# A norm without GpSimd, and an FFN's first pair without a modulation step

## The chip, the cores and the metric

The kernel runs on one core of a Trainium2 chip. The metric is the device time of one execution in microseconds, as the median of three runs. Matrix products run on TensorE (PE), elementwise work on VectorE (DVE), ScalarE (ACT) and GpSimd (POOL); SyncE (SP) issues all the DMA transfers.

## The reference, cut to what matters

Two layers transform 512 image tokens and 256 context tokens of width 1024. Each layer has three sublayers (FFN, token mixer, FFN), and each starts with a norm whose result is scaled and shifted by vectors that come from a condition `c`:

```python
mod = (cond_lat @ w_ada[layer] + b_ada[layer])     # 9 vectors of 1024 for each layer
y = x * rsqrt(mean(x * x) + 1e-6) * norm_w
y = y * (1 + scale) + shift                        # modulate
h = h + 0.5 * gate * (silu(y @ w_gate) * (y @ w_up)) @ w_ffn_out   # FFN, width 2816
```

The mixer holds a Fourier mix, retention, and window attention between two more products. All is float32. `w_ada` is 1024 x 9216 for each layer, and must be read and multiplied too, for the image's and for the context's condition.

## The kernel before, in words

**Layout.** Features lie on the 128 partitions and tokens along them: `h` is 8 tiles (k = 0 to 7) of 128 features x 768 tokens. A float32 product is made of three fast ones: each operand is split into a high part (`xhi`, `whi`, rounded by a cast) and the rest (`xlo`, `wlo`), and `xhi*whi + xlo*whi + xhi*wlo` is summed in PSUM. So every weight tile passes through a chain: DMA to `raw`, ScalarE's cast to `whi` (`split_hi`, L1005), VectorE's subtraction to `wlo` (`split_lo`, L1309), and only then TensorE (`unit`, L637). Weights come in pairs of units (slots 0 and 1). An FFN is done in two halves: an "in" phase of 11 pairs (a gate unit and an up unit), then an "out" phase of 4 pairs; the mixer has a "win" phase of 8 pairs, its own middle part, and a "wo" phase of 4.

**Norms.** There are six, norm 0 to norm 5; norms 0, 2, 3 and 5 lead into an FFN, norms 1 and 4 into a mixer. Each is done in two parts of tokens (0 to 511 and 512 to 767; 256 and 256 in norm 5), each part in 8 tiles. For each tile GpSimd multiplies `h` by `rstd` into `tnorm` (two buffers), ScalarE computes scale and shift into `xfull` (two buffers) and, for even k of part 0, a second time into `xhi`; for the other tiles VectorE casts `xhi` from `xfull` (L1441). VectorE subtracts to `xlo` (L1442). Four hand-overs through two-deep buffers for each tile, then. TensorE's first pair behind a norm (`first_pair`, L704) takes the tiles in as they come (semaphore `s_xn`): tile by tile, three matmuls for each unit. Between them VectorE also adds the last tiles of the sublayer before (L1423), sums their squares (L1432), and splits the first weights.

**Modulation steps.** The 144 tiles of `w_ada` products are spread over the kernel in 64 steps of two (after 16 tiles that are done at the start); `ADA_PAIRS` says at which pairs. A step is: SP loads eight transfers into the four pieces of `ada` (`load_ada`, L478), VectorE sums 16 products (`sum_ada`, L1385 and L1388), and at the end of the pair TensorE folds them over the partitions (`ada_fold`, L652). Two of the four pieces lie where `tnorm` and `xfull` are, so behind a norm SP waits for its last `xlo` before it loads those (`norm_done`).

**Order.** Each engine runs its own list in the order written, and SP's transfers are issued in order too. Nothing but the semaphores ties the engines together. SP issues the step's transfers before the next pair's weights.

## Time and profile before

| | us |
|---|---|
| median of 3 runs (lowest to highest) | 2910.24 (2910.11 to 2912.97) |
| the profiled execution | 2913.79 |
| its span, first to last instruction | 2912.0 |
| TensorE busy in it | 2778.7 (95%) |
| VectorE, ScalarE, GpSimd busy | 1594.4, 740.9, 199.3 |
| mean granted TensorE clock | 0.978 |

A row of the timeline has its start and duration in us from the span's start, then engine, line, operation, output <- inputs, and in brackets how long the engine had been idle and which instruction ended that. A duration covers a pipelined instruction from end to end, so neighbours may overlap. PEclk 1.00 is the full TensorE clock. "ns" is said where it is meant. Norm 2 is the one shown in detail: its first root is taken at 1027 us.

### The profile page before, as it was taken

The numbers are of one execution on the slowest core, as the hardware profiler recorded it, in microseconds if no ns is written. First come the engines' busy times: TensorE is split into PE (matmuls) and PEld (weight loads), VectorE is DVE, ScalarE is ACT, GpSimd is POOL, SyncE is SP. The second block draws the span as 40 slices with busy tenths as digits, with TensorE's granted clock in tenths as the row PEclk, the third lists the DMA queues.
The fourth block names the chain that finished last, engine by engine and source line by source line (L and its number), as shares of the span: only waits on it lengthen the run. The fifth ranks groups of instructions, "written<-read, shape, count | busy, mean of one in ns | idle before, by whom it ended". The sixth has DMA issues, their size and how long they took to land.

```text
span 2912.0 us, 41929 instructions
## 1 busy us (share of the span) xinstructions
PE 2778.7 (95%) x15315; PEld 2352.0 (81%) x15315; DVE 1594.4 (55%) x2687; ACT 740.9 (25%) x1107; POOL 199.3 (7%) x151
## 2 busy tenths in 40 slices
PE   6899999989999979999999799999998999899998
PEld 4788888878749868888888688888886839788887
DVE  5676377453458467734773677347336457533333
ACT  4111111132337231111111311111114246422222
POOL 2000000020131020000000200000002041200000
PEclk8999999999999989999999899999999999999999
DMA  7777377313100147725771477357222300233232
GB/s 223 189 180 175 93 187 187 98 39 101 51 1 1 48 103 187 187 64 146 181 174 57 107 174 180 87 125 186 69 67 82 77 15 1 58 99 103 87 106 88
DMA packets 485788, 319.29 MB, mean 110 GB/s; under 512 B 30588, under 2 KB 481488, under 8 KB 485712
## 3 DMA queue, kind: packets, MB, share of 16 engines
q1 hardware_dynamic: 485712, 318.29, 42.8%
q8 instruction: 45, 0.74, 0.1%
q14 instruction: 31, 0.25, 0.0%
HBM read 316.14 MB, written 2.10 MB: 109 GB/s over the span
## 4 chain that ended last, share of the span: by engine, by line
PE 89%; DVE 6%; ACT 2%; DMA 1%; issue 1%; SPq 1%; DVEq 0%; ACTq 0%
PE pg L637 76%; PE pg L704 3%; PE p L913 2%; DVE xlo L1442 2%; PE pn L897 1%; DVE xhi L1441 1%; PE p L652 1%; PE p L843 1%; PE pg L843 1%; PE pg L866 1%; DMA raw<-in_ffn_w_in 1%; DVE wlo L1309 1%; DVE part L1388 1%; ACT xfull L1083 0%; PE pn L788 0%
## 5 line engine op out<-in xcount | busy, mean ns | idle before, releaser
L637 PE MATMUL pg<-xhi,whi 128*128 128x512 f32 x2880 | 805.0, 348 | 8.4 <-DVE wlo L1309 6.4
L637 PE MATMUL pg<-xhi,wlo 128*128 128x512 f32 x2880 | 800.6, 346 | 0.0
L637 PE MATMUL pg<-xlo,whi 128*128 128x512 f32 x2880 | 798.9, 346 | 0.0
L1005 ACT CAST whi<-raw 128x1024 fp32r<-128x1024 f32 (+1 forms) x288 | 321.7, 1117 | 1096.6 <-PE pg L637 1068.9
L1309 DVE TENSOR_TENSOR wlo<-raw,whi 128x1024 fp32r<-128x1024 f32 (+1 forms) x288 | 382.5, 1328 | 372.4 <-ACT whi L1005 369.7
L637 PEld LDWEIGHTS pg<-xhi,whi 128*128 128x128 f32 x2880 | 459.1, 190 | 78.1 <-DVE wlo L1309 6.9
L637 PEld LDWEIGHTS pg<-xlo,whi 128*128 128x128 f32 x2880 | 457.2, 189 | 70.5
L637 PEld LDWEIGHTS pg<-xhi,wlo 128*128 128x128 f32 x2880 | 457.5, 189 | 69.9
L1388 DVE SCALAR_TENSOR_TENSOR part<-ada,cond,part 128x256 f32<-128x256 f32 x960 | 465.2, 485 | 32.7
L1473 DVE SCALAR_TENSOR_TENSOR h<-pg,gcol,h 128x512 f32 (+1 forms) x118 | 71.4, 639 | 463.7 <-PE pg L637 463.7
L637 PE MATMUL pg<-ahi,wlo 128*128 128x512 f32 x1100 | 306.9, 347 | 0.0
L637 PE MATMUL pg<-ahi,whi 128*128 128x512 f32 x1100 | 306.7, 347 | 0.0
L637 PE MATMUL pg<-alo,whi 128*128 128x512 f32 x1100 | 306.2, 346 | 0.0
L597 POOL TENSOR_TENSOR tnorm<-h,rstd 128x256 f32<-128x256 f32 (+1 forms) x96 | 113.2, 1199 | 1942.4 <-ACT rstd L1070 1900.6
L1242 ACT ACTIVATE gate<-pg 128x768 f32<-128x768 f32 (+1 forms) x88 | 66.8, 759 | 595.1 <-PE pg L637 594.1
L637 PEld LDWEIGHTS pg<-ahi,whi 128*128 128x128 f32 x1100 | 174.6, 188 | 27.8
L637 PEld LDWEIGHTS pg<-ahi,wlo 128*128 128x128 f32 x1100 | 174.5, 188 | 27.5
L637 PEld LDWEIGHTS pg<-alo,whi 128*128 128x128 f32 x1100 | 174.2, 188 | 27.8
L1636 DVE TENSOR_TENSOR gate<-gate,pg 128x768 f32<-128x768 f32 (+1 forms) x88 | 78.1, 887 | 148.4 <-PE pg L637 146.6
L704 PE MATMUL pg<-xhi,whi 128*128 128x256 f32 (+1 forms) x240 | 92.4, 385 | 38.3 <-DVE xlo L1442 38.0
L704 PEld LDWEIGHTS pg<-xhi,whi 128*128 128x128 f32 x240 | 50.8, 212 | 57.7 <-DVE xlo L1442 37.0
L704 PE MATMUL pg<-xlo,whi 128*128 128x256 f32 (+1 forms) x240 | 85.1, 355 | 0.0
(201 smaller groups left out, 2346.1 us busy)
## 6 DMA issues: line engine op xcount, KB each, us to landing
ada<-in_w_ada SPq DMA_DIRECT2D x512, 256.0 KB, 4.2
raw<-in_ffn_w_in SPq DMA_DIRECT2D x176, 512.0 KB, 3.9
raw<-in_ffn_w_out SPq DMA_DIRECT2D x64, 704.0 KB, 4.6
raw<-in_w_in SPq DMA_DIRECT2D x24, 512.0 KB, 3.9
ada_first<-in_w_ada SPq DMA_DIRECT2D x8, 1024.0 KB, 11.9
dft_sb<-in_dft SPq DMA_DIRECT2D x2, 2048.0 KB, 9.7
raw<-in_w_in SPq DMA_DIRECT2D x16, 256.0 KB, 3.5
raw<-in_w_o SPq DMA_DIRECT2D x16, 256.0 KB, 2.8
```

Source lines behind the costliest of these rows:

```text
L597: nc.gpsimd.tensor_tensor(tnorm[:, k % 2, p0:p1], h[:, k, p0:p1], rstd[:, p0:p1], ALU.mult).then_inc(s_t, 1)
L637: last = nc.tensor.matmul(pg[s][:, p0:p1], w[:, s, k], v[:, k, p0:p1], start=(k == 0 and n == 0), stop=(k == kt - 1 and n == 2))
L704: last = nc.tensor.matmul(pg[s][:, c0:c0 + p1 - p0], w[:, s, k], v[:, k, p0:p1], start=(k == 0 and n == 0), stop=(k == kt - 1 and n == 2))
L843: last = nc.tensor.matmul(o[p0:p0 + HD, 0:SEQ], w, sdec[:, r % 2, 0:SEQ], start=(jt == 0), stop=(jt == ret_blocks - 1))
L913: last = nc.tensor.matmul(pa[q // 2 % 2][:, s * HD:(s + 1) * HD], probT[:, q % 2, j * P:(j + 1) * P], vatt[:, kt, s * HD:(s + 1) * HD], st ...
L1005: nc.scalar.copy(whi[:, s, 0:nk], raw[:, s, 0:nk]).then_inc(s_whi[s], 1)
L1242: nc.scalar.activation(gate[:, 0:t], pg[0][:, 0:t], ACT.Silu).then_inc(s_free[0], 1)
L1309: nc.vector.tensor_sub(wlo[:, s, 0:nk], raw[:, s, 0:nk], whi[:, s, 0:nk].bitcast(f32)).then_inc(s_w[s], 1)
L1388: ins = nc.vector.scalar_tensor_tensor(part[:, :], ada[q][:, a], cond2[:, n:n + 1], part[:, :], ALU.mult, ALU.add)
L1442: nc.vector.tensor_sub(xlo[:, k, p0:p1], xfull[:, k % 2, p0:p1], xhi[:, k, p0:p1].bitcast(f32)).then_inc(s_xn, 1)
L1473: last = nc.vector.scalar_tensor_tensor(hv, pg[s][:, p0:p1], gcol[:, col, v:v + 1].rearrange("p o v -> p (o v)"), hv, ALU.mult, ALU.add)
L1636: nc.vector.tensor_tensor(gate[:, 0:t], gate[:, 0:t], pg[1][:, 0:t], ALU.mult).then_inc(s_free[1], 1)
```

## The change

The table of modulation steps has new counts, and no step lies in an FFN's first pair (64 steps as before; it starts one pair later, one step more lies in the first out phase, two more in the last in phase). SP loads the second pair's weights before it waits for the norm. In the norm GpSimd does nothing. VectorE multiplies `h` by the scale column and `rstd` in one instruction into `tnorm` (four buffers now), ScalarE adds the shift and rounds into `xhi`, and VectorE computes `tnorm + shift - xhi` into `xlo` in one instruction. VectorE's list has the next tile's scaling ahead of each `xlo`, and the weights' splits and the adds stand later in it. `xfull` is left for the squares alone.

```diff
-ADA_PAIRS = {(0, 0, 0): (16, 11, 2), (0, 0, 1): (42, 11, 0), (0, 1, 0): (64, 11, 0),
-             (0, 1, 1): (86, 11, 0), (1, 0, 0): (108, 11, 0), (1, 0, 1): (130, 7, 0)}
+ADA_STEPS = {(0, 0, 0): (16, 10, 3), (0, 0, 1): (42, 11, 0), (0, 1, 0): (64, 10, 0),
+             (0, 1, 1): (84, 11, 0), (1, 0, 0): (106, 10, 0), (1, 0, 1): (126, 9, 0)}
...
-        tnorm = place("tnorm", [P, 2, TOK], f32, m0 + TOK * 4)
+        tnorm = place("tnorm", [P, 4, TOK], f32, m0 + TOK * 4)
...
-                    if q == 2 and norm_done is not None:
-                        sp.wait_ge(s_xn, norm_done)
...
-                        elif kind == "in" and hf == 0 and a == 0:
+                            continue
+                        if kind == "in" and hf == 0 and a == 0:
                             load_step(0, b, layer)
-                            a = 1
+                            continue
+                        if kind == "in" and hf == 0 and a == 1 and b is not None:
+                            load_step(1, None, layer)
+                            sp.wait_ge(s_xn, xn_count(m, 1, KD - 1))
+                            load_ada(b, 1, layer)
+                            a = 2
...
-                    pool.wait_ge(s_r, 2 * m + part_ + 1)
-                    for k in range(KD):
-                        if k >= 2:
-                            pool.wait_ge(s_xf, xn_count(m, part_, k - 2))
-                        nc.gpsimd.tensor_tensor(tnorm[:, k % 2, p0:p1], h[:, k, p0:p1], rstd[:, p0:p1], ALU.mult
-                                                ).then_inc(s_t, 1)
...
                             first_pair(i, t)
-                            if b is not None:
-                                ada_fold(b, 0)
                             a = 1
...
-                    for dst in (xfull[:, k % 2, p0:p1], xhi[:, k, p0:p1])[:1 if vector_high(part_, k) else 2]:
-                        last = nc.scalar.activation(dst, tnorm[:, k % 2, p0:p1], ACT.Identity,
-                                                    bias=mod[:, shift + k, v:v + 1], scale=acol[:, k, v:v + 1])
+                    nc.scalar.activation(xhi[:, k, p0:p1], tnorm[:, k % 4, p0:p1], ACT.Identity,
+                                         bias=mod[:, shift + k, v:v + 1]).then_inc(s_xh, 1)
...
+                def scaled(part_, k):
+                    ...
+                    nc.vector.scalar_tensor_tensor(tnorm[:, k % 4, p0:p1], h[:, k, p0:p1], acol[:, k, v:v + 1],
+                                                   rstd[:, p0:p1], ALU.mult, ALU.mult).then_inc(s_t, 1)
                 def low(part_, k):
-                    if vector_high(part_, k):
-                        link(nc.vector.tensor_copy(xhi[:, k, p0:p1], xfull[:, k % 2, p0:p1]))
-                    nc.vector.tensor_sub(xlo[:, k, p0:p1], xfull[:, k % 2, p0:p1], xhi[:, k, p0:p1].bitcast(f32)
-                                         ).then_inc(s_xn, 1)
+                    nc.vector.scalar_tensor_tensor(xlo[:, k, p0:p1], tnorm[:, k % 4, p0:p1],
+                                                   mod[:, shift + k, v:v + 1], xhi[:, k, p0:p1].bitcast(f32),
+                                                   ALU.add, ALU.subtract).then_inc(s_xn, 1)
...
                 for k in range(2, KD):
+                    if k + 1 < KD:
+                        scaled(0, k + 1)
                     low(0, k)
+                scaled(1, 0)
                 for k in range(KD):
+                    if k + 1 < KD:
+                        scaled(1, k + 1)
                     low(1, k)
```

On SP's list, behind the wo phase ahead of norm 2 (`raw` takes weights, `ada_57` to `ada_60` are the four pieces of a step; the wait for the norm stands inside). Before:

```order
L491 DMA raw<-in_ffn_w_in 128x8x128 x2
L478 DMA ada_57<-in_w_ada 64x4x256 x2
L478 DMA ada_58<-in_w_ada 64x4x256 x2
L478 DMA ada_59<-in_w_ada 64x4x256 x2
L478 DMA ada_60<-in_w_ada 64x4x256 x2
L538 UNCONDITIONAL_BRANCH
```

and now:

```order
L487 DMA raw<-in_ffn_w_in 128x8x128 x4
L474 DMA ada_57<-in_w_ada 64x4x256 x2
L474 DMA ada_58<-in_w_ada 64x4x256 x2
L474 DMA ada_59<-in_w_ada 64x4x256 x2
L474 DMA ada_60<-in_w_ada 64x4x256 x2
L538 UNCONDITIONAL_BRANCH
```

The weights of the second pair (two more `raw` transfers) have moved from behind the branch to ahead of the step's eight, and ahead of the wait for the norm.

On VectorE's list, at the start of a norm's first part (here norm 1; norms 2 to 5 have the same order). Before:

```order
L1423 SCALAR_TENSOR_TENSOR h<-pg,gcol,h 128x256
L1432 TENSOR_TENSOR rstd<-rstd,xfull 128x256
L1309 TENSOR_TENSOR wlo<-raw,whi 128x1024
L1423 SCALAR_TENSOR_TENSOR h<-pg,gcol,h 128x256
L1442 TENSOR_TENSOR xlo<-xfull,xhi 128x512
L1432 TENSOR_TENSOR rstd<-rstd,xfull 128x256
L1441 CAST xhi<-xfull 128x512
L1442 TENSOR_TENSOR xlo<-xfull,xhi 128x512
L1309 TENSOR_TENSOR wlo<-raw,whi 128x1024
L1442 TENSOR_TENSOR xlo<-xfull,xhi 128x512
```

and now:

```order
L1405 SCALAR_TENSOR_TENSOR h<-pg,gcol,h 128x256
L1429 SCALAR_TENSOR_TENSOR tnorm<-h,acol,rstd 128x512 x2
L1437 SCALAR_TENSOR_TENSOR xlo<-tnorm,mod,xhi 128x512
L1291 TENSOR_TENSOR wlo<-raw,whi 128x1024
L1429 SCALAR_TENSOR_TENSOR tnorm<-h,acol,rstd 128x512
L1437 SCALAR_TENSOR_TENSOR xlo<-tnorm,mod,xhi 128x512
L1414 TENSOR_TENSOR rstd<-rstd,xfull 128x256
L1405 SCALAR_TENSOR_TENSOR h<-pg,gcol,h 128x256
L1291 TENSOR_TENSOR wlo<-raw,whi 128x1024
L1414 TENSOR_TENSOR rstd<-rstd,xfull 128x256
L1429 SCALAR_TENSOR_TENSOR tnorm<-h,acol,rstd 128x512
L1437 SCALAR_TENSOR_TENSOR xlo<-tnorm,mod,xhi 128x512
```

Each tile has two three-operand instructions on VectorE now (`tnorm`, L1429, and `xlo`, L1437) in place of a subtraction and, for most tiles, a cast; the first sum of squares and the first `wlo` have moved behind the first tiles, and the last add behind the second `xlo`.

## Rows read from the trace of the kernel before

**Rows 1.** The page: busy us (share) and instructions by engine.
```profile
PE 2778.7 (95%) x15315; PEld 2352.0 (81%) x15315; DVE 1594.4 (55%) x2687; ACT 740.9 (25%) x1107; POOL 199.3 (7%) x151
```

**Rows 2.** All waits: who <- whom: us in total, times, longest.
```profile
PE pg L704 <- DVE xlo L1442: 38.0, 34, 4.3
...
PE p L652 <- DVE part L1388: 34.5, 3, 11.8
```

**Rows 3.** PE in norm 2: start us, us, what [idle before <- releaser].
```profile
1040.20 0.79 PE L704 MATMUL pg<-xhi,whi 128*128 128x512 f32 x1 [0.33 <-DVE xlo L1442]
...
1050.88 0.39 PE L704 MATMUL pg<-xlo,whi 128*128 128x512 f32 x1
1051.10 0.39 PE L704 MATMUL pg<-xhi,wlo 128*128 128x512 f32 x1
...
1060.34 0.28 PE L704 MATMUL pg<-xhi,wlo 128*128 128x256 f32 x1
1072.39 1.01 PE L652 MATMUL p<-consts,part 128*128 128x2 f32 x4 [11.77 <-DVE part L1388]
```

**Rows 4.** Timeline of PE, behind norm 0.
```profile
80.64 1.02 PE L652 MATMUL p<-consts,part 128*128 128x2 f32 x4 [11.06 <-DVE part L1388]
```

**Rows 5.** Timeline of SP's queue, end of norm 2.
```profile
1057.09 2.58 SPq L478 DMA_DIRECT2D ada<-in_w_ada  x4
1060.02 1.06 SPq L491 DMA_DIRECT2D raw<-in_ffn_w_in  x2
```

**Rows 6.** Timeline of ACT, norm 2 and behind it.
```profile
1027.56 0.63 ACT L1070 ACTIVATE rstd<-rstd 128x512 f32<-128x512 f32 x1
...
1057.78 0.81 ACT L1242 ACTIVATE gate<-pg 128x768 f32<-128x768 f32 x1 [0.20 <-PE pg L704]
1065.99 1.04 ACT L1005 CAST whi<-raw 128x1024 fp32r<-128x1024 f32 x1 [7.40 <-DMA raw<-in_ffn_w_in]
```

**Rows 7.** Timeline of DVE, norm 2 and behind it.
```profile
1032.04 0.47 DVE L1423 SCALAR_TENSOR_TENSOR h<-pg,gcol,h 128x256 f32<-128x256 f32 x1
1032.43 1.36 DVE L1442 TENSOR_TENSOR xlo<-xfull,xhi 128x512 fp32r<-128x512 f32 x1
...
1056.64 0.42 DVE L1442 TENSOR_TENSOR xlo<-xfull,xhi 128x256 fp32r<-128x256 f32 x1
...
1067.07 1.23 DVE L1309 TENSOR_TENSOR wlo<-raw,whi 128x1024 fp32r<-128x1024 f32 x1 [6.09 <-ACT whi L1005]
```

**Rows 8.** DVE by line and form, whole run: busy us, mean ns | idle.
```profile
L1388 DVE SCALAR_TENSOR_TENSOR part<-ada,cond,part 128x256 f32<-128x256 f32 x960 | 465.2, 485 | 32.7
...
L1442 DVE TENSOR_TENSOR xlo<-xfull,xhi 128x512 fp32r<-128x512 f32 x40 | 47.5, 1194 | 5.8 <-ACT xhi L1083 5.1
...
L1423 DVE SCALAR_TENSOR_TENSOR h<-pg,gcol,h 128x512 f32<-128x512 f32 x8 | 6.0, 750 | 31.6 <-PE pg L704 31.6
```

**Rows 9.** Windows: us; busy us (x) PE, PEld, DVE, ACT, POOL; PEclk, DMA, GB/s.
```profile
1073.40:1092.40 19.00, 19.00 (x102) 16.70 (x102) 11.62 (x22) 1.97 (x3) 0.00 (x0) 0.89 0.79 174
1092.40:1109.50 17.10, 17.10 (x102) 15.01 (x102) 12.37 (x23) 2.80 (x4) 0.00 (x0) 1.00 0.76 185
2541.00:2549.20 8.20, 7.52 (x36) 7.21 (x37) 3.79 (x8) 4.01 (x5) 0.64 (x1) 0.58 0.02 6
```

**Rows 10.** Timeline of DVE, the last of norms 0, 1 and 5.
```profile
64.82 0.42 DVE L1442 TENSOR_TENSOR xlo<-xfull,xhi 128x256 fp32r<-128x256 f32 x1
...
68.24 0.18 DVE L1376 TENSOR_SCALAR lgb<-lg 128x16 f32<-128x16 f32 x1
...
655.36 0.43 DVE L1442 TENSOR_TENSOR xlo<-xfull,xhi 128x256 fp32r<-128x256 f32 x1
...
2543.30 0.43 DVE L1442 TENSOR_TENSOR xlo<-xfull,xhi 128x256 fp32r<-128x256 f32 x1
```

**Rows 11.** Timeline of PE, resume behind norm 4.
```profile
2236.31 0.79 PE L637 MATMUL pg<-xhi,whi 128*128 128x512 f32 x1 [6.44 <-DVE wlo L1309]
```

**Rows 12.** Timeline of ACT, the root of norm 5.
```profile
2521.46 0.42 ACT L1070 ACTIVATE rstd<-rstd 128x256 f32<-128x256 f32 x1
```

More of the change, by code:

```diff
@@ L379, in sq_count @@
             return base + n + 1 + (2 * part if m and n >= KD - 2 else 0)
-        def vector_high(part, k):
-            return part == 1 or k % 2 == 1
         def coef_count(m, k):
@@ L400, in ada_runs @@
             kind, l, m, hf = phases[i][:4]
-            b, first_pairs, second_pairs = ADA_PAIRS.get((l, m % 3 // 2, hf), (0, 0, 0))
-            count = {"in": first_pairs, "out": second_pairs}.get(kind, 0)
-            if kind == "out":
-                b += 2 * first_pairs
+            b, in_steps, out_steps = ADA_STEPS.get((l, m % 3 // 2, hf), (0, 0, 0))
+            skip = 1 if kind == "in" and hf == 0 else 0
+            count = {"in": in_steps, "out": out_steps}.get(kind, 0)
+            b += 2 * (in_steps if kind == "out" else 0) - 2 * skip
             runs, at = [], 0
-            while at < min(count, n):
+            if skip:
+                runs, at = [(0, 1, None, l)], 1
+            while at < min(count + skip, n):
                 layer = (b + 2 * at) // MT
-                end = min(count, n, ((layer + 1) * MT - b) // 2)
+                end = min(count + skip, n, ((layer + 1) * MT - b) // 2)
                 runs.append((at, end, b, layer))
@@ L505, in load_step @@
                         if b is not None:
[L506 removed]
+                            load_ada(b, f, layer)
                 elif kind == "out":
```

72 lines of the change are left out of this document (37 added, 35 removed).

## The prediction

> **What bounds the kernel now.** I read the page's busy times first: TensorE works 2778.7 us of a span of 2912.0 [rows 1], so it is the bound, and only what makes it wait or slows its clock can be won. The view of all waits then names who holds it up: `xlo` of the norms, 38.0 us in 34 waits, and three waits of a fold for VectorE's sums, 34.5 us together [rows 2]. Both lie at the norms, so I read norm 2 as a timeline, engine by engine.
>
> Its root is ready at 1027.56 + 0.63 = 1028.19 [rows 6]. The first `xlo` ends at 1033.79 [rows 7]; TensorE waits for tiles until 1040.20 and has no break from there to part 1 [rows 3]; the last `xlo` ends at 1056.64 + 0.42 = 1057.06 [rows 7], 28.9 us behind the root, and TensorE ends the first pair at 1060.6. Then it stands still for 11.77 us until the fold [rows 3]. Why: two pieces of the step wait for the norm's last `xlo`, so SP issues them at 1057.09, and the second pair's weights behind them at 1060.02 [rows 5]. ScalarE is done with the gate at 1058.59 and waits 7.40 us for those weights [rows 6]; VectorE waits 6.09 us in the middle of the step's sums for ScalarE [rows 7], and TensorE waits for the sums. Behind norm 0 it is the same, 11.06 us [rows 4], and the third of the three waits, behind norm 3, is what is left of the 34.5: 11.7. In the stretch after it, the same pair of units takes 19.0 us at a mean clock of 0.89, against 17.1 at 1.00 one pair later [rows 9]: the idle time costs clock too, 1.9 us.
>
> **The change, part by part.** *No step in the first pair, weights early.* The second pair's weights are issued as soon as their slots are free, some 20 us ahead of need. After the first pair nothing is late but the chain gate, cast, subtraction. With the norm as it was: gate to 1058.59, cast 1.04, subtraction 1.23 [rows 6, 7], with hand-overs 1061.0, against 1073.40 now: 12.4 us, and 1.9 us of clock. Is the sum late in the next pair instead? There the eight transfers start at the norm's end as two pieces do now, and from that point to the fold is 1072.39 - 1057.09 = 15.3 us now, 6 to 7 of them the wait for the weights, which is gone. The fold will come due one pair (17.1 us) plus 3 to 4 us after that point. It is in time.
>
> *The norm.* VectorE now does all but ScalarE's one instruction of a tile. Price of the new two-tensor instruction: 256 columns took 0.485 us with both tensors in SBUF, 512 took 0.750 with one in PSUM [rows 8]. Bounds: 0.69 us or a little less for 512 below, and above the 1.194 that `xlo` takes in the mean now [rows 8]. That mean holds waits for GpSimd: the same 512 columns took 1.36 us at 1032.43 while GpSimd wrote `tnorm`, and with GpSimd gone nothing of that kind is left. I take 0.75 and 0.485. Instructions follow each other closer than they last: 0.47 long, 0.39 apart [rows 7], so 0.67 and 0.40 for each. Norm 2: 16 x 0.67 + 16 x 0.40 = 17.1; two `wlo` at 1.15 = 2.3; two sums and an add = 1.1; about 1 us of waiting at the start, while ScalarE writes the first `xhi` behind a weight cast. Together 21.5 us from the root to the last `xlo`, against 28.9. ScalarE needs some 0.75 us for a tile, below VectorE's 1.34, so it is hidden; in part 1 its tile of 256 columns is near VectorE's 0.80 and may cost a few tenths. TensorE needs 1.36 us for a tile of part 0 (six matmuls 0.22 to 0.23 apart [rows 3]), as VectorE does, so neither gains by being faster still. Last `xlo` at 1049.8, then TensorE's last 27 matmuls, which end 3.5 us behind it now (1060.34 + 0.28, about 0.12 apart [rows 3]): 1053.2. The chain for the second pair starts when the first unit is done, and ends at about 1053.5. Against 1073.40 that is 19.9 us, with the clock 21.8.
>
> *The same for the others.* Norm 3 is norm 2 with a wait of 11.7: 21.6. Norm 1 has norm 2's pattern (last `xlo` 655.36 + 0.43 [rows 10]) and no step behind it: 7.4 us on the `xlo`, some of the half-speed tail besides: 8. Norm 4 does not use part 1 in its first pair, but VectorE must finish it before it splits the next weights: TensorE waits 6.44 us there and resumes at 2236.31 [rows 11]. With the norm 7.2 us shorter and the same chain behind it: 6.7. Norm 5 has only tiles of 256 columns: 32 x 0.40 + 2.3 + 1.1 + 1.0 = 17.2 us from its root at 2521.88 [rows 12], so 2539.1 against 2543.73 [rows 10]; TensorE's tail ran at a clock of 0.58 up to 2549.2 [rows 9]. 6.2 us, some of it clock. Norm 0 waits for the modulation's own folds and transfers in part 0, so only part 1 shortens, about 2 us (last `xlo` at 65.24 now [rows 10]). Behind it VectorE works on the decays, to 68.42 [rows 10], now 2 us earlier, and only then splits the second weights: TensorE resumes at 68.6 and not behind the fold at 81.5 [rows 4]. 12.9 us, and 2 of clock: 15.
>
> *What is added.* Three folds move from a wait to full pairs; a fold lasts 1.01 us behind a wait [rows 3] and, at the full clock and with its neighbours overlapped, half of that or less: -1.5. VectorE's 8 us of sums for a step lie in pairs where it is busy 12.4 of 17.1 us with them [rows 9], so they are hidden. In an out phase a pair lasts 23 us, more room still.
>
> Sum: 15 + 8 + 21.8 + 21.6 + 6.7 + 6.2 = 79.3; less 1.5 = 77.8. I take 4 us off, because in part 1 TensorE will still wait for each tile, and its tail may run at half clock after it, as in norm 5 (27 matmuls 0.21 apart in place of 0.12 are 2.4 us, in one or two norms). So 74. The profiled execution took 2913.79, which makes 2840; the median of the runs lies 3.5 us lower: **2836 us**.
>
> **Clock, by the page.** In norm 5's tail the granted clock is 0.58 after the waits for tiles, behind the fold's wait 0.89 over a pair [rows 9]. The Trainium skill (TensorE: Matmul & The Clock Gate, "HAM oscillation — how this bites in real kernels") says that a kernel whose bursts of matmuls are divided by waits falls back to the low clock again and again. The trace agrees in kind. By that rule part 0 could stay at 1.2 GHz throughout, which speaks against the norm's half of the gain; it is rival A.
>
> **Rivals.**
> *A: the norm's supply is faster, but TensorE is not.* The new order has longer waits at the start (the third `xlo` stands behind two sums, an add and two splits), then tiles at just TensorE's pace. If it takes them at 1.2 GHz, a tile of part 0 costs 2.6 us in place of 1.36, the norm's part 0 lasts as long as now, and only a us is won at each norm. The stall still goes: 12.4 + 1.9 twice and 14 at norm 0 are 43; + 6 - 1.5 = 47, so 2863. For it: rows 9. Against: from 1040.20 to part 1 TensorE put 14 of 16 tiles and units through in 11 us with nothing to wait for [rows 3], and at 1050.88 its matmuls were 0.22 apart, the full rate.
> *B: the wait only moves.* The second pair's fold finds its sums late, because eight transfers (2 MB) and the third pair's weights now come together at the norm's end. Then 9 of 12 us return each time: 77.8 - 27 - 5 of clock = 45, so 2865. Against: the margin of 5 us above.
> *C: slower.* VectorE as the only supplier is too slow. If an instruction with two tensors and a column ran in two passes, 1.4 us for 512 and 0.9 for 256, each norm would take 17 us more than I sum up, 100 in all: 2936. It decides from 77.8 / 6 = 13 us a norm, which is about 1.25 us for 512 columns. Against: 960 such instructions at 485 ns [rows 8]. The Trainium skill (VectorE: DVE Perf Modes, "The perf-mode tier table") has a copy in float32 at twice the rate of a two-tensor operation, and casts are what is given up here; by it the new instruction is at 691 ns for 512 columns, if it goes as a plain addition does. That would shorten my sum by 1 us a norm.
> *D: it doesn't do what it says:* the second weights stay late because of their slots. Then only the norms gain, about 40: 2870. By VectorE's list each slot is free with the first pair's `wlo`, early in part 0, so I give it little.
>
> **How the numbers follow.** Forecast 0.75, A 0.12, B 0.07, C 0.03, D 0.03. The forecast's own range is 2824 to 2850: below, norm 0 better by 3, norms better by 1 to 2 each (the 691 ns); above, an instruction 0.1 us longer (3 us a norm in the large ones) or two more tails at half clock. With half of A and B the range for 8 in 10 is 2822 to 2860. A measurement of this kernel tells 0.2% (6 us) from no change. All cases but C are faster by more: faster 0.96, same 0.01, slower 0.03.
>
> **What would show it.** In the new profile no fold waits for `part` at the three places, and the second pair starts within 1 us of the first pair's end behind norms 1, 2, 3 and 5, within 3 behind norm 0 and 4. `xlo` from `tnorm` takes 0.7 to 0.75 us for 512 columns with no spread; root to last `xlo` 21 to 22 us in norms 1 to 4. Waits of TensorE on `xlo` fall from 38 to some 20 us. PEclk in the pair behind norm 2 is above 0.95. The forecast is wrong if a tile takes VectorE above 1.6 us, if a fold waits in the second pair, or if PEclk stays near 0.5 through part 0.

## The result, and the profile after

The changed kernel took 2838.96 us (median of 4 runs, 2828.34 to 2840.37), the kernel before 2910.39 (2910.11 to 2912.97): a ratio of 0.9745, 95% interval 0.9721 to 0.9769. The forecast was 2836. Taken once more with the third set of experiments below it was 2836.73 (5 runs, 2834.78 to 2838.03), against 2912.44 for the kernel before in the same set: 0.9738 (0.9724 to 0.9751). One run of experiment e3 took 8713.7 us at a mean granted clock of 0.308; it is in no comparison, and its cause is open.

The profiled execution was the fastest of all nine, 2828.34 us with a span of 2826.2. Its page, busy times as in [rows 1]:

```profile
PE 2752.1 (97%) x15315; PEld 2330.4 (82%) x15315; DVE 1567.6 (55%) x2711; ACT 715.6 (25%) x1083; POOL 86.1 (3%) x55
```

GpSimd's norm products are gone from it (199.3 before), and VectorE, which took over work, is busy 27 us less than before. TensorE does the same 15315 matmuls and stands still less. It also needs less time for them: 2778.7 us became 2752.1 (2756.7 in the repeat), while the mean granted clock rose from 0.978 to 0.992 (0.991). So of the 85.8 us by which the span is shorter (78.1 in the repeat) 26.6 (22.0) are shorter matmuls, and the rest are shorter waits. Its waits, in the columns of [rows 2]:

```profile
PE pg L690 <- DVE xlo L1437: 7.1, 18, 1.2
...
PE pg L623 <- DVE wlo L1291: 6.0, 5, 3.6
PE pn L684 <- DVE rstd L1414: 5.8, 5, 1.6
...
PE pg L690 <- DVE wlo L1291: 3.2, 2, 2.1
```

Waits for `xlo` fell from 38.0 to 7.1 us, and no wait for `part` is left of 34.5. What is left at the norms is short: weights, the second part's sum of squares, the first weights of norm 2.

VectorE's new instructions by form (busy us, mean ns | idle), to be held against [rows 8]:

```profile
L1437 DVE SCALAR_TENSOR_TENSOR xlo<-tnorm,mod,xhi 128x512 fp32r<-128x512 f32 x40 | 29.9, 746 | 2.9 <-ACT xhi L1063 1.6
L1429 DVE SCALAR_TENSOR_TENSOR tnorm<-h,acol,rstd 128x512 f32<-128x512 f32 x40 | 29.4, 745 | 1.9 <-ACT rstd L1056 1.8
L1437 DVE SCALAR_TENSOR_TENSOR xlo<-tnorm,mod,xhi 128x256 fp32r<-128x256 f32 x56 | 26.8, 480 | 2.8 <-ACT xhi L1063 2.8
L1429 DVE SCALAR_TENSOR_TENSOR tnorm<-h,acol,rstd 128x256 f32<-128x256 f32 x56 | 26.2, 478 | 0.9 <-ACT rstd L1056 0.9
```

The forecast took 0.75 and 0.485 us, and they are 0.746 and 0.480. In the profile of before the old `xlo` alone took 1.194 in the mean for 512 columns [rows 8].

Norm 2 engine by engine, as [rows 3, 5, 6, 7] show it for before. First ScalarE's root, then VectorE's last `xlo`, then TensorE's first chunk and second pair, then SP's queue:

```profile
997.24 0.63 ACT L1056 ACTIVATE rstd<-rstd 128x512 f32<-128x512 f32 x1
```

```profile
1018.77 0.48 DVE L1437 SCALAR_TENSOR_TENSOR xlo<-tnorm,mod,xhi 128x256 fp32r<-128x256 f32 x1 [0.18 <-ACT xhi L1063]
```

```profile
1001.41 0.76 PE L690 MATMUL pg<-xhi,whi 128*128 128x512 f32 x1 [2.06 <-DVE wlo L1291]
...
1023.11 0.62 PE L623 MATMUL pg<-xhi,whi 128*128 128x512 f32 x2 [0.30 <-DVE wlo L1291]
```

```profile
1001.38 3.55 SPq L487 DMA_DIRECT2D raw<-in_ffn_w_in  x2
1019.28 5.26 SPq L474 DMA_DIRECT2D ada<-in_w_ada  x8
```

From the root's end at 997.87 the last `xlo` comes at 1019.25, 21.4 us later (28.9 before), and the second pair at 1023.11, 25.2 us later. Before, the fold alone stood 44.2 us behind the root (1072.39 - 1028.19), and the second pair 45.1. The second pair's weights are issued at 1001.38, 18 us ahead of the last `xlo`; what waits for the norm's end is only the next step's eight transfers.

The windows (columns of [rows 9]) give the clock: TensorE's first chunks of norm 2, the rest of its start, then short stretches in norms 1, 3 and 4, and last the pair behind norm 2 and the tail of norm 5:

```profile
1001.40:1003.80 2.40, 2.39 (x6) 1.63 (x6) 2.40 (x5) 0.36 (x2) 0.00 (x0) 0.52 0.48 138
1003.80:1006.00 2.20, 1.27 (x4) 0.30 (x2) 2.20 (x4) 1.10 (x3) 0.00 (x0) 0.75 0.34 102
...
619.20:622.60 3.40, 3.40 (x10) 2.63 (x9) 3.40 (x6) 2.59 (x5) 0.00 (x0) 0.50 0.00 0
1574.90:1578.30 3.40, 3.12 (x7) 2.51 (x8) 3.40 (x6) 2.43 (x5) 0.00 (x0) 0.50 0.15 43
2155.20:2162.00 6.80, 5.64 (x13) 4.46 (x14) 2.33 (x2) 1.28 (x2) 0.00 (x0) 0.50 1.00 332
```

```profile
1023.10:1040.60 17.50, 17.49 (x100) 15.23 (x100) 12.38 (x22) 2.88 (x4) 0.00 (x0) 1.00 1.04 222
...
2455.00:2463.00 8.00, 7.44 (x55) 6.55 (x53) 5.46 (x13) 5.57 (x9) 0.00 (x0) 1.00 0.00 0
```

The pair behind the norm runs at the full 2.4 GHz (0.89 of it before), and so does norm 5's tail (0.58 before). Half clock is left for one or two short stretches at each norm: at norm 2's start, 10 us behind the roots of norms 1 and 3, and around the wait behind norm 4. The place is not the same in each execution. In the repeat the same wait of 2.06 us stands at norm 2's start (its root ends at 1006.29), and the clock stays full for another 6 us before it falls:

```profile
1009.80:1015.70 5.90, 3.59 (x11) 1.75 (x11) 5.90 (x10) 2.13 (x4) 0.00 (x0) 1.00 0.55 162
1015.80:1019.10 3.30, 3.10 (x7) 2.48 (x8) 3.30 (x6) 2.35 (x5) 0.00 (x0) 0.50 0.07 21
```

The simplest book-keeping of the gain is from one norm's root to the next. The root's end is the row above, and the same row of the other norms; here those of norms 1, 3 and 4 in the profiled run of the changed kernel, then norms 1 to 4 in the profiled run of its repeat:

```profile
608.43 0.63 ACT L1056 ACTIVATE rstd<-rstd 128x512 f32<-128x512 f32 x1
...
1564.78 0.63 ACT L1056 ACTIVATE rstd<-rstd 128x512 f32<-128x512 f32 x1
...
2132.05 0.63 ACT L1056 ACTIVATE rstd<-rstd 128x512 f32<-128x512 f32 x1
```

```profile
611.66 0.63 ACT L1056 ACTIVATE rstd<-rstd 128x512 f32<-128x512 f32 x1
...
1005.66 0.63 ACT L1056 ACTIVATE rstd<-rstd 128x512 f32<-128x512 f32 x1
...
1573.06 0.63 ACT L1056 ACTIVATE rstd<-rstd 128x512 f32<-128x512 f32 x1
...
2139.98 0.63 ACT L1056 ACTIVATE rstd<-rstd 128x512 f32<-128x512 f32 x1
```

| from root to root, us | before | after | gain | repeat | gain |
|---|---|---|---|---|---|
| start to norm 0's | 35.90 | 35.02 | 0.9 | 37.90 | -2.0 |
| 0 to 1 (holds norm 0) | 590.75 | 574.04 | 16.7 | 574.39 | 16.4 |
| 1 to 2 (norm 1, the mixing) | 401.54 | 388.81 | 12.7 | 394.00 | 7.5 |
| 2 to 3 (norm 2) | 589.92 | 567.54 | 22.4 | 567.40 | 22.5 |
| 3 to 4 (norm 3) | 587.34 | 567.27 | 20.1 | 566.92 | 20.4 |
| 4 to the end (norms 4, 5) | 706.55 | 693.52 | 13.0 | 693.29 | 13.3 |
| span | 2912.0 | 2826.2 | 85.8 | 2833.9 | 78.1 |

The stretches from norm 0's root to norm 1's and from norm 2's root to the end agree to 0.4 us between the two executions of one program. The 8 us by which the first profile is faster lie at the start and in the stretch that holds the mixing. Since the same program has them in one execution and not in the other, they are no part of what the change does.

### The profile page after: what moved, and what is told of

Same layout as the page of the kernel before. It is cut to its first block, busy times and chain, and to the rows that moved or that the text cites. A ratio compares the mean times of both kernels' runs of the same rounds, so it can differ in the third digit from the quotient of the medians.

```text
span 2826.2 us, 41817 instructions
## 1 busy us (share of the span) xinstructions
PE 2752.1 (97%) x15315; PEld 2330.4 (82%) x15315; DVE 1567.6 (55%) x2711; ACT 715.6 (25%) x1083; POOL 86.1 (3%) x55
## 4 chain that ended last, share of the span: by engine, by line
PE 92%; DVE 3%; ACT 2%; issue 1%; SPq 1%; DMA 1%; DVEq 0%; ACTq 0%
PE pg L623 77%; PE pg L690 4%; PE p L899 2%; PE pn L883 1%; DVE xlo L1437 1%; PE pg L829 1%; PE p L829 1%; PE p L638 1%; DVE tnorm L1429 1%; PE pg L852 1%; PE pn L774 1%; PE pg L774 0%; SPq L521 0%; ACT whi L991 0%; DVE wlo L1291 0%
## 5 line engine op out<-in xcount | busy, mean ns | idle before, releaser
L623 PEld LDWEIGHTS pg<-xhi,whi 128*128 128x128 f32 x2880 | 455.5, 188 | 77.2 <-DVE wlo L1291 7.5
L690 PE MATMUL pg<-xhi,whi 128*128 128x256 f32 (+1 forms) x240 | 86.1, 359 | 10.5 <-DVE xlo L1437 7.1
L1646 DVE TENSOR_TENSOR alo<-gate,ahi 128x768 f32 (+3 forms) x88 | 78.5, 892 | 9.7
L587 POOL TENSOR_TENSOR rk_st<-z,rk_st 64x768 fp32r<-64x768 f32 x8 | 16.8, 2103 | 2175.9 <-ACT rq_hi L1102 2175.7
L690 PE MATMUL pg<-xlo,whi 128*128 128x256 f32 (+1 forms) x240 | 81.4, 339 | 0.0
## 6 DMA issues: line engine op xcount, KB each, us to landing
ada_first<-in_w_ada SPq DMA_DIRECT2D x8, 1024.0 KB, 11.8
```

The source lines that it names most:

```text
L623: last = nc.tensor.matmul(pg[s][:, p0:p1], w[:, s, k], v[:, k, p0:p1], start=(k == 0 and n == 0), stop=(k == kt - 1 and n == 2))
L690: last = nc.tensor.matmul(pg[s][:, c0:c0 + p1 - p0], w[:, s, k], v[:, k, p0:p1], start=(k == 0 and n == 0), stop=(k == kt - 1 and n == 2))
L1646: nc.vector.tensor_sub(lo, gate[:, 0:t], hi.bitcast(f32)).then_inc(s_a[m, hf], 1)
```

## The experiments

Twelve runs in four sets; the kernel before ran in each (2911.11, 2911.58, 2912.44, 2910.56 us), and every time is set against the one of its own set. All edits are to the changed kernel unless it is said.

**e1, the new norm alone.** The norm of the change (GpSimd out, four `tnorm`, VectorE's two instructions) with the modulation steps, SP's order and TensorE's fold in the first pair of the kernel before:

```diff
-ADA_STEPS = {(0, 0, 0): (16, 10, 3), ...
+ADA_PAIRS = {(0, 0, 0): (16, 11, 2), ...
...
+                    if q == 2 and norm_done is not None:
+                        sp.wait_ge(s_xn, norm_done)
```

> The new norm alone; the modulation steps stay where they were in the kernel before (a step in each FFN's first pair, its second half loaded behind the norm, the second pair's weights behind that). Theory: in the kernel before the fold in norm 2 started 15.3 us after the norm's last xlo, and the second pair 1 us later; both move with the last xlo, so a faster norm keeps its whole gain. In the changed kernel the second pair starts 3.9 us after the last xlo. So this kernel is slower than the changed one by 12.5 us at each of three norms, 37.5 in all, with about 2 for the slower clock behind the waits: 2877 to 2881, about 31 under the kernel before, with three fold waits of 11 to 12 us. Rival: the fold waits swallow the norm's gain in norms 0, 2 and 3 (they are set by the transfers and not by the last xlo), which leaves norms 1, 4 and 5: 21 us of gain, 2889.

2871.20 us (2867.3 to 2874.06): 39.9 under before, ratio 0.9868 (0.9851 to 0.9885). The three fold waits stand, with their length unchanged:

```profile
PE p L634 <- DVE part L1364: 35.5, 3, 12.0
```

So the wait follows the last `xlo` and does not swallow the norm's gain; the rival (2889) is out. The expected gain was too small by 9: the stretches from root to root gain 5.4 at norm 0, 12.0, 9.6 and 10.2 at norms 1, 2 and 3, where VectorE's 7.4 us alone was counted; the rest was not counted, and it is not placed. The stretch of norm 1 holds the mixing, which differs by 5 us between two executions of one program (table above). And by e1's page a part of this half's gain lies in the matmuls themselves: TensorE is busy 2756.5 us in it, 22.2 less than before, and in e2 (below) 2780.8, no less at all.

**e2, the new steps alone.** The kernel before with the new table, SP's order and no fold in the first pair; its norm as it was. 

> The new modulation steps alone (none in an FFN's first pair, the second pair's weights loaded during the norm); the norm is that of the kernel before, with GpSimd's products. Theory: the second pair starts 3.9 us after the last xlo and not 16.4, three times: 37.5 us, and 2 to 4 for the slower clock behind the waits: 2869 to 2872, no fold wait for part. The two halves add up to the whole of 71.4 us. Rival: the halves overlap or need one another, and this one alone gains under 30 us.

2875.91 us (2874.85 to 2881.45): 35.2 under before, ratio 0.988 (0.9864 to 0.9895). No wait for `part` is left. 35.2 and e1's 39.9 make 75.1; both together gave 71.4 and 75.7. The halves add, to within what two sets differ by. The time is 4 to 7 us above what was expected: from root to root the stretches of norms 0, 2 and 3 gave 11.0, 14.0 and 12.3 us in its profile, which is of the slowest of its four runs, and not 14 each.

**e3, early weights with the fold left in the first pair.** e1 with the second pair's weights issued ahead of the wait for the norm's end:

```diff
                     if q == 2 and norm_done is not None:
+                        if ahead is not None:
+                            ahead()          # load_step(1, None, layer)
                         sp.wait_ge(s_xn, norm_done)
```

> The new norm with the old modulation steps (e1), but the second pair's weights are issued ahead of the wait for the norm's end, as in the changed kernel; only the step's second half and the next step's pieces stay behind it. Theory: in the step VectorE splits the second pair's weights between the step's two halves, so late weights delay the fold too. With early ones the fold follows the transfer of the two pieces (some 5 us) and eight sums (some 4): about 10 us after the last xlo instead of 15.3. The fold wait falls from 11.8 to about 6 us, three times: 2860 to 2865, 16 to 20 us under e1. Rival: the fold waits for the modulation pieces and sums alone, the weights are hidden behind them, and nothing changes against e1.

2859.57 us (2852.88 to 2862.84, three runs): 51.5 under before, ratio 0.9819 (0.9794 to 0.9843), 11.6 under e1. The fold waits:

```profile
75.76 1.01 PE L642 MATMUL p<-consts,part 128*128 128x2 f32 x4 [9.17 <-DVE part L1372]
...
1042.17 1.01 PE L642 MATMUL p<-consts,part 128*128 128x2 f32 x4 [5.61 <-DVE part L1372]
...
1617.25 1.02 PE L642 MATMUL p<-consts,part 128*128 128x2 f32 x4 [4.69 <-DVE part L1372]
```

At norms 2 and 3 they are 5.6 and 4.7 instead of 12.0 and 11.7, as the theory had it. VectorE's lists show it: in e1 it stood 6.30 us for `whi` in the middle of the sums, here it goes on:

```profile
1035.62 3.61 DVE L1364 SCALAR_TENSOR_TENSOR part<-ada,cond,part 128x256 f32<-128x256 f32 x7
1045.53 1.22 DVE L1285 TENSOR_TENSOR wlo<-raw,whi 128x1024 fp32r<-128x1024 f32 x1 [6.30 <-ACT whi L987]
```

```profile
1033.00 3.61 DVE L1372 SCALAR_TENSOR_TENSOR part<-ada,cond,part 128x256 f32<-128x256 f32 x7
1036.52 1.22 DVE L1293 TENSOR_TENSOR wlo<-raw,whi 128x1024 fp32r<-128x1024 f32 x1
```

Norm 0's wait lost only 2.7 of 11.8, where 6 were expected, and not all of the shorter waits came through: the stretches of norms 2 and 3 are 5.3 and 3.1 us shorter from root to root than e1's, with waits shorter by 6.4 and 7.1. The clock behind a wait of 4.7 us was as low as behind one of 11.7 (0.86 and 0.91 over a pair), so a wait cut to half costs its tail all the same; the rest has no row. So half or more of the fold wait at norms 2 and 3 was late weights, by way of VectorE's list.

**e4, late weights without the fold.** The other way round:

```diff
-                            load_step(1, None, layer)
                             sp.wait_ge(s_xn, xn_count(m, 1, KD - 1))
+                            load_step(1, None, layer)
                             load_ada(b, 1, layer)
```

> The changed kernel, with the second pair's weights issued behind the wait for the norm's end instead of ahead of it; still no step in the first pair. Theory: the weights are then issued at the last xlo, take 3 to 5 us to land and 2.2 to be split, and the second pair starts 6 to 8 us after the last xlo and not 3.9: 2 to 4 us more at each of three norms, 2845 to 2851. Rival: only the step in the first pair mattered, and this kernel takes what the changed one does, 2839.

2842.86 us (2842.55 to 2849.23), ratio 0.9772 (0.9757 to 0.9788): 3.9 over the changed kernel's first set and 6.1 over its repeat, 2 us under the shortest time that was expected. The second pair waits for `wlo` 2.74, 2.60 and 2.33 us behind norms 0, 2 and 3, in place of 1.61, 0.30 and 0.22. So SP's order alone is worth 4 to 6 us by the medians once no fold stands there, and some 12 while one does (e3 against e1). The profiled run, 4.9 us over this kernel's median, has more: its stretches of norms 0, 2 and 3 are 11.8 us longer than the repeat's.

**e5, GpSimd beside the norm.** GpSimd multiplies 256 columns into scratch, in step with the norm; nothing waits for it. The edit does so in norms 1 to 4 (96 instructions, 97 us), not in norm 5 as its text says; in the kernel before, the norm products took 113 us in six norms:

```diff
+                        for _ in range(2 - part_):
+                            nc.gpsimd.tensor_tensor(scratch, dist_sb[:, 0:256], consts[:, 0:256], ALU.mult
+                                                    ).then_inc(s_beside, 1)
```

> The changed kernel, with GpSimd multiplying tiles of 256 columns into a scratch tile during norms 1 to 5 (two for each chunk of a norm's first part, one in the second, each behind the last chunk's low part); nothing waits for it. Theory: what the change takes off VectorE's path is the time in which both engines read SBUF: in the kernel before the low parts of 512 columns took 0.69 to 1.8 us, mean 1.19, beside GpSimd's products, here 0.74 to 0.75. So VectorE's instructions in the norms grow to about 1.0 to 1.2 us while GpSimd runs, the last xlo comes 4 to 6 us later after the root than 21.4, and the kernel takes 12 to 25 us more, 2851 to 2864. Rival: VectorE's and GpSimd's instructions don't hinder one another, the spread of before was a wait for tnorm and xfull inside the record, and this kernel takes 2839.

2872.23 us (2867.83 to 2875.99), ratio 0.9869 (0.9854 to 0.9884): 39.4 under before, so 36 of the change's 75.7 are gone through an engine that nobody waits for. VectorE and GpSimd in norm 2 (from its root to its last `xlo`, 31.2 us in place of 21.4):

```profile
L1453 DVE SCALAR_TENSOR_TENSOR tnorm<-h,acol,rstd 128x512 f32<-128x512 f32 x8 | 8.8, 1110 | 1.8 <-ACT rstd L1080 1.8
L1461 DVE SCALAR_TENSOR_TENSOR xlo<-tnorm,mod,xhi 128x512 fp32r<-128x512 f32 x8 | 8.7, 1099 | 0.0
L1461 DVE SCALAR_TENSOR_TENSOR xlo<-tnorm,mod,xhi 128x256 fp32r<-128x256 f32 x8 | 7.1, 893 | 0.0
```

```profile
L603 POOL TENSOR_TENSOR cond<-dist_sb,consts 128x256 f32<-128x256 f32 x24 | 24.3, 1012 | 112.0 <-ACT rstd L1080 104.6 <-DVE xlo L1461 6.1
```

The direction was right and the size too small by half: 0.745 us became 1.10, 0.480 became 0.6 to 0.9, 10 us a norm. Norm 5, without the extra GpSimd work, keeps its 0.480. The rival (no hindrance) is out. What in the chip makes the one engine slow the other is not shown by this run.

**e6, another order in norms 1 to 5.** TensorE takes `whi*xhi` as soon as `xhi` is there and `xlo` last, both halves chunk by chunk; VectorE splits the first weights ahead of `xlo`:

```diff
+                for n, (w, v) in enumerate(((whi, xhi), (wlo, xhi), (whi, xlo))):
...
+                    if s == 0 and n != 1:
+                        pe.wait_ge((s_xh, s_xh, s_xn)[n], xn_count(m, part_, k))
...
+                        order = ahead + [(s, k) for k in range(len(ahead) // 2, KD) for s in range(2)]
```

> The changed kernel with another order in norms 1 to 5: TensorE starts a chunk on whi*xhi as soon as xhi is there and needs xlo only for the third product; the two halves of a pair alternate by chunk; VectorE splits the first weights ahead of xlo's first chunk, and does the second part's squares one chunk later. Theory: from the root on, TensorE had 17.2 us of products left and ended 24.9 to 26.1 us after the root in norms 2 and 3, though the last xlo came after 21.4; the rest is waits at the start (2.1, 0.6, 0.6, 0.4 us in norm 2; 1.2 us for the sum of squares in the others) and the half with s=1 that runs behind the last xlo. The first pair's end comes to 22 us after the root: 2.5 to 4 us in each of norms 1, 2 and 3, 1 in 5, none in 4: 8 to 12 us, 2827 to 2831. Rival: VectorE sets the end in any order, only the last 0.5 to 1 us of TensorE can be taken, and the gain is under 4 us.

2835.47 us (2832.49 to 2836.9), ratio 0.9736 (0.9723 to 0.9749): 76.1 under before, where the changed kernel is 75.7 under it. No gain that can be told. The first pair did get shorter as the theory had it, and its clock stays at 1.00 through all of norm 2's first pair (window of this run, columns as above), where the changed kernel had a stretch at half clock. The second window is the start of the second pair:

```profile
1003.00:1025.20 22.20, 20.16 (x111) 16.37 (x109) 20.77 (x37) 14.02 (x24) 0.00 (x0) 1.00 0.16 49
1027.10:1033.80 6.70, 5.55 (x17) 4.78 (x18) 6.49 (x10) 0.78 (x1) 0.00 (x0) 0.50 1.12 234
```

It ended 22.2 us behind the root. But then:

```profile
1028.25 1.01 PE L623 MATMUL pg<-xhi,whi 128*128 128x512 f32 x2 [3.02 <-DVE wlo L1302]
```

Root to second pair is 25.3 us, the 25.2 of the changed kernel to a tenth. And the half clock is not saved, it has moved behind this wait: the third pair starts 45.2 us behind the root, against 42.8 and 43.7 in the two profiles of the changed kernel. With both halves ending together the first weight slot comes free only at the pair's end, and ScalarE's table load and Silu, its cast and VectorE's subtraction follow, which the half with s=1 had hidden before:

```profile
1023.90 1.28 ACT L1233 ACT_TABLE_LOAD   x1
1025.19 0.81 ACT L1233 ACTIVATE gate<-pg 128x768 f32<-128x768 f32 x1
1025.90 1.98 ACT L1003 CAST whi<-raw 128x1024 fp32r<-128x1024 f32 x2
```

The time speaks for the rival, the reason was another: the start of the second pair is set by the chain behind the last `xlo`, and not by TensorE's order in the first pair.

**e7, second weights split earlier.** In norm 4 they are split between the norm's two parts, in norm 0 ahead of the decays:

```diff
+                    norm(i - 1, m, (lambda: (evict(0), evict(1))) if early else None)
...
+                    if between is not None and k in (0, 2):
+                        between(k // 2)          # split_lo(i, s, 1)
```

> The changed kernel with the second pair's weights split earlier where TensorE waited for them: in norm 4 between the norm's two parts (the first two tiles take the first part alone), in norm 0 ahead of the decays. Theory: the two waits for wlo of 3.6 and 1.6 us go, 4 to 5 us in all: 2834 to 2835. Rival: the wait in norm 4 is the norm's second part by another name; VectorE's 6.6 us of it then come before the third pair, and it only moves.

2837.95 us (2836.73 to 2846.93), ratio 0.9745 (0.9732 to 0.9759): nothing gained. The wait behind norm 4 went and the one behind norm 0 fell from 1.62 to 0.31 us, and a new one came before norm 4's third pair:

```profile
2186.62 0.80 PE L623 MATMUL pg<-xhi,whi 128*128 128x512 f32 x1 [11.99 <-DVE wlo L1299]
```

SP's queue names it: the third pair's weights stand behind the norm's end, the rope table and the transform table (2 MB):

```profile
2172.33 0.37 SPq L545 DMA_DIRECT2D rope_sb<-in_rope  x1
2172.74 0.47 SPq L547 DMA_DIRECT2D dft_sb<-in_dft  x1
2173.25 5.32 SPq L487 DMA_DIRECT2D raw<-in_w_in  x2
```

The profiled run (2846.93) is the slowest of the five, 9 us over the median. So the trace shows where the wait comes from, but how long it is in the other four runs isn't known.

**e8, e6 and e7 together.**

> Both edits of e6 and e7 in one kernel. Theory: they touch different waits and add up: 12 to 16 us under the changed kernel, 2823 to 2827. Rival: in norm 4 both take the same wait, and the sum falls short by 2 to 3 us.

2842.89 us (2838.59 to 2843.15), ratio 0.9757 (0.9744 to 0.977), 7 above e6 and 5 above e7, where 12 to 16 under the changed kernel were expected. Each of the two brought its own new wait (3.0 us for `wlo` behind norms 2 and 3, 9.2 before norm 4's third pair), and both stayed.

**e9, e6 mended by its trace.** The half with s=1 runs one chunk behind in the second part; in the first step the weights are split ahead of Silu; the decays stand behind that step:

```diff
+                        if first:
+                            split_hi(nxt, 0, jn)
                         nc.scalar.activation(gate[:, 0:t], pg[0][:, 0:t], ACT.Silu).then_inc(s_free[0], 1)
-                        split_hi(nxt, 0, jn)
+                        if not first:
+                            split_hi(nxt, 0, jn)
```

> e6 with three changes where its trace showed the new wait: in the second part TensorE's half with s=1 runs one chunk behind the half with s=0 (not beside it), so the first weight slot comes free with the last chunk; ScalarE splits the second pair's weights before it takes the gate's Silu in the first step; the decays stand behind the first step. Theory: what sets the second pair's start is the chain last xlo, last chunk with s=0 (0.4), weights split by ScalarE (1.04) and VectorE (1.2), about 2.8 us instead of the 3.9 of the changed kernel and the same of e6, where Silu (0.8) stood in it: 1 us in five norms, and 1.6 in norm 0: 2830 to 2834. Rival: the transfer of the weights or the end of the half with s=1 takes its place, and the time is e6's, 2835.

2831.05 us (2829.21 to 2838.37), ratio 0.9723 (0.9709 to 0.9738): 5.7 under the changed kernel of the same set, as forecast in size (the two intervals overlap, so the difference is only just to be told), but not where: root to second pair at norm 2 is still 25.3 us, now waiting for the gate:

```profile
1026.68 0.86 PE L623 MATMUL pg<-xhi,whi 128*128 128x512 f32 x2 [2.71 <-ACT gate L1235]
```

```profile
1023.37 1.05 ACT L1004 CAST whi<-raw 128x1024 fp32r<-128x1024 f32 x1 [1.12 <-PE pg L697]
1024.43 1.28 ACT L1235 ACT_TABLE_LOAD   x1
1025.73 0.81 ACT L1235 ACTIVATE gate<-pg 128x768 f32<-128x768 f32 x1
```

ScalarE's table load had lain in a wait and now lies in the chain. By the roots 3.9 us are norm 0's (570.5 us from its root to norm 1's, against 574.4). Part of that can be scatter: e5, whose norm 0 is the changed kernel's, has 571.6 there. The rest can't be placed, since the profiled run (2836.99) was 6 us over this kernel's median. A table load placed behind the last `xhi` could take up to 1.3 us out of this chain at norms 2, 3 and 5, an estimate from the row of its 1.28 us; that was not tried.

**e10, two passes.** VectorE's first instruction of a chunk done as two:

```diff
-                    nc.vector.scalar_tensor_tensor(tnorm[:, k % 4, p0:p1], h[:, k, p0:p1], acol[:, k, v:v + 1],
-                                                   rstd[:, p0:p1], ALU.mult, ALU.mult).then_inc(s_t, 1)
+                    link(nc.vector.tensor_tensor(tn, h[:, k, p0:p1], rstd[:, p0:p1], ALU.mult))
+                    nc.vector.tensor_scalar(tn, tn, acol[:, k, v:v + 1], None, ALU.mult).then_inc(s_t, 1)
```

> The changed kernel with VectorE's first instruction of each chunk, (h*acol)*rstd, done as two: h*rstd, then times acol, each waiting for the one before. Theory: from the root to the last xlo VectorE is the bound, so each us that it gets there is a us of the kernel. A tensor_tensor of 512 columns takes 0.69 us and a tensor_scalar of 256 columns 0.35 against 0.48 for the scalar_tensor_tensor; with the wait between, a chunk of 512 columns costs about 0.65 more and one of 256 about 0.36: 8 us more at norms 1 to 4, 5 to 6 at norms 0 and 5: 35 to 44 us, 2874 to 2883, and root to last xlo 29 to 30 us where it was 21.4. Rival: the first pair's products hide VectorE's surplus, and under 20 us of it show.

2868.62 us (2866.04 to 2871.61), ratio 0.9848 (0.9833 to 0.9863): 31.9 over the changed kernel of the same set. Root to last `xlo` is 27.2 us in norms 1 to 4, 5.8 more (the tensor_scalar of 512 columns took 0.486 us, the next instruction began 0.40 behind it, and a chunk cost less than the 0.65 counted). From root to root the stretches of norms 0 to 3 are 6.8, 4.3, 6.9 and 3.3 us longer than in the changed kernel's repeat, and norms 4 and 5 together 10.6: what VectorE needs more comes out at the end. The rival (under 20) is out, and the forecast's case C is measured at a third of its strength.

**e11, the changed kernel again.**

> The changed kernel once more, as it is, beside the others of this call. Theory: its profiled run (2828.3 us) was 10 us under its other three (2838.4 to 2840.4); the norms' stretches of e4, e6 and e7 take the same time as there while the stretch from norm 1's root to norm 2's took 388.8 us there and 391 to 398 in these, so the difference is TensorE's spacing of matmuls from run to run and no property of the kernel: median 2838 to 2840, with single runs from 2828 to 2843. Rival: 2828 is what the kernel takes when nothing disturbs it, and comes again in half of the runs.

2836.73 us (2834.78 to 2838.03); root to root in the table above. The median is 1 to 3 us under what was expected, and 2828 did not come again in these five runs, against the rival.

**e12, e9 with norm 4 as in e7 and the third pair's weights ahead of the tables.**

```diff
+                            for n_ in ahead:              # (4, 5) in the last layer
+                                load_win(n_)
                             sp.wait_ge(s_xn, xn_count(m, 1, KD - 1))
...
+                        if early and n in (2, 3):
+                            split_lo(i, s, 2)             # ahead of the rope
```

> e9 with norm 4 done as in e7 (the second pair's weights split between the norm's parts) and with what e7's trace showed behind it removed: the third pair's weights are loaded ahead of the wait for the norm's end and of the rope table, and split ahead of the rope. Theory: the wait of 6.1 us for wlo behind norm 4 goes without coming back before the third pair (12.0 us in e7): 5 to 6 us under e9's 2831, so 2825 to 2827. Rival: VectorE is late by the norm's second part whatever stands first, the wait only moves to the third or fourth pair, and the time is e9's or more.

2826.40 us (2825.58 to 2833.8), ratio 0.9722 (0.9708 to 0.9737): 84.2 under the kernel before in its set. e9 was 81.4 under the one in its own, so the medians alone do not tell the two apart (the ratios are 0.9722 and 0.9723). The traces do: from norm 4's root to norm 5's it takes 304.0 us, against 310.5 in e9 and 309.3 in the changed kernel's repeat. The wait behind norm 4 is 1.52 us (6.11 in e9), and none over 1.2 stands before the third pair:

```profile
2153.41 0.50 PE L629 MATMUL pg<-xhi,whi 128*128 128x512 f32 x1 [1.52 <-DVE wlo L1321]
```

This is the fastest of all versions: 84.2 us under before, where the changed kernel is 71.4 and 75.7 under it.

## Why the prediction was right, step by step

**The steps' half.** That the fold's wait hangs on the last `xlo`, and that VectorE's wait for the weights lies in it, is shown by e1 (same waits behind an earlier `xlo`) and e3 (weights early, 12.0 to 5.6 and 11.7 to 4.7). The step was priced at 12.4 us and 1.9 of clock at norms 2 and 3, and 14 at norm 0, some 42 in all. That is too much: e2 has this half at 35.2, and the whole less e1 leaves 31.5 (first set) or 35.8 (repeat), so it is worth no more in the changed kernel. In e2's trace the third pairs behind norms 0, 2 and 3 start 11.5, 14.0 and 12.8 us earlier, counted from the root, 38.3 together; the rest of the difference is not placed. Rival B (the wait moves to the next fold) has no row: no fold waits for `part` in the changed kernel.

**The norm's half.** VectorE's sum was 21.5 us from root to last `xlo`; it took 21.4, with the prices taken (0.75 and 0.485 against 0.746 and 0.480). e10 shows that this path sets the time nearly us for us: root to last `xlo` is 34.5 us longer over the six norms than in the repeat, and the kernel 31.9. The low price against the old mean of 1.194 us rested on GpSimd's absence, and e5 bears that out: with a GpSimd that only multiplies into scratch the new instructions take 1.10. Such a GpSimd costs 36 of the 75.7 us, and what is left, 39.4 under before, is hardly more than the new steps give with the old norm (e2, 35.2). So by these two runs, of different sets, the larger part of the norm's half is that engine's silence. The other parts (four buffers, one write of ScalarE in place of two, VectorE's new order) were not tried one by one. This half was priced too low: the sum has some 36 us for it (79.3 less 43), and e1 gave 39.9. Counted from the root to the next undisturbed pair, e1's trace has 4.1 us at norm 0, where 2 were forecast, and 8.0, 7.7, 8.1, 7.2 and 6.2 at norms 1 to 5.

**Luck in the total.** The steps' half was some 6 us too high and the norm's half some 4 us too low, and the two nearly cancel. The mechanisms are the forecast's; that the total came so close, 2836 against 2838.96 and 2836.73, is in part luck.

The prediction also quotes 691 ns for a plain addition of 512 columns as what the new instruction might cost. In the Trainium skill (VectorE: DVE Perf Modes) that figure stands in the section "The TRN2 errata — SBUF-src ops pay a fixed extra latency per instruction", not in the table it names. The trace agrees with it for a plain two-tensor instruction (e10's `tensor_tensor` took 0.686 us in the mean); the new instruction took 0.746. So the microsecond a norm that the prediction held possible from it did not come.

**By norms.** Predicted 15, 8, 21.8, 21.6, 6.7 and 6.2 = 79.3. Measured from the root to the next undisturbed pair (in norms 0, 2 and 3 the third pair, in the others the second), before against changed: 15.9, 6.8, 21.3, 20.6, 7.2 and 6.2 = 78.0; with the repeat's profile 16.8, 6.3, 20.4, 20.9, 7.2 and 6.2 = 77.8. At norm 0 the chain behind the decays left a wait of 1.61 us, as foreseen:

```profile
67.49 0.62 PE L623 MATMUL pg<-xhi,whi 128*128 128x512 f32 x2 [1.61 <-DVE wlo L1291]
```

**What was off.** The 4 us taken off for tails at half clock were not there: norm 5's tail ran at 1.00, and in the profile TensorE's waits for `xlo` are 7.1 us (7.9 in the repeat) and not "some 20". Half clock showed earlier, in the first parts of the norms and behind norm 4 (the windows above), for which the sum had no term. The repeat's profile has the sum: 78.1 us of span, against 77.8 without that deduction. The medians differ by 71.4 and 75.7, so the deduction helped the number by chance: no row speaks for the reason it was made for. The wait behind norm 4 is 3.62 us (3.80 in the repeat), above the 3 that the text allowed:

```profile
2156.36 0.79 PE L623 MATMUL pg<-xhi,whi 128*128 128x512 f32 x1 [3.62 <-DVE wlo L1291]
```

**Rival A** (TensorE at 1.2 GHz through part 0) did not hold: no norm's part 0 stayed at half clock, and all of TensorE's waits for `xlo` came to 7.1 us. What there is of it is one short stretch in a part 0, 3.4 us long in the windows of norms 1 and 3, with 0.52 and 0.75 at norm 2's start. The Trainium skill (TensorE: Matmul & The Clock Gate, "HAM oscillation — how this bites in real kernels") says that bursts of matmuls divided by waits fall back to the low clock again and again. The trace agrees in kind, once or twice at each norm. One wait's length does not tell where: behind the same 2.06 us the clock was 0.52 in the first profile and 1.00 in the repeat.

**Rival C** (VectorE too slow, 2936) turned on a price that did not hold; e10 gives what such a price costs, 32 us for 5.8 us a norm in norms 1 to 4, so 17 a norm would have cost over 90 us, an estimate in proportion. **Rival D** has its own measurement in e4: with late weights the kernel would have lost 4 to 6 us of its gain by the medians, not 34. The late weights did their harm mostly through the sums in the first step (e3 against e1, 11.6 us), and those are gone.

## What to carry to other kernels

When an engine waits for a sum, look in the list of the engine that makes it for what else stands there: here the modulation's fold waited for weights, because the split of late weights stood between two halves of the sum. An engine can slow another one's instructions without any wait between them (e5), so taking it out can give back more than its own place in the chain; price the instructions that are left by clean rows of the same kind, not by their mean beside the other engine. And a wait removed by reordering is worth nothing until the next chain to the same point is known: e6, e7 and e8 each removed waits and got new ones elsewhere, and only the versions that followed each new wait's row (e9, e12) came out below the changed kernel.

## What the runs showed of the hardware beyond that

- GpSimd tensor_tensors of 256 columns (1.01 us each, 24.3 of the 31.2 us of e5's norm 2) slow VectorE's instructions of 512 columns from 0.745 to 1.10 us in the mean, though they share no data; 256 columns from 0.480 to 0.59 (`tnorm`) and 0.89 (`xlo`).
- VectorE's scalar_tensor_tensor cost as much from SBUF alone (0.746) as with one operand in PSUM (0.750 [rows 8]); instructions behind each other start 0.66 and 0.40 us apart.
- Behind the same 2.06 us of idle time TensorE's next matmuls ran at a granted clock of 0.52 (2.4 us) in one execution and at 1.00 (5.9 us) in another of the same program; there the fall to 0.50 came 6 us later.
- ScalarE's table load took 1.28 us, and the Silu behind it began 0.02 us after its end (e9).
- One program took 388.8 and 394.0 us for the same stretch in two executions (root of norm 1 to root of norm 2), and agreed to 0.4 us in the others behind norm 0's root. A difference of 5 us between two single profiles says nothing here.
